# Another order of K chunks behind the norms, two equal column groups for the indexer, and its key's layer norm elsewhere

## The chip, the core and the metric

The kernel runs on one core of a Trainium2 chip. The metric is the device time of one execution in microseconds (us). TensorE (PE) multiplies, VectorE (DVE), ScalarE (ACT) and GpSimd (POOL) do the rest, and SyncE (SP) issues nearly all transfers. The engines run their own instruction lists and meet at semaphores.

## What is computed

Two blocks over 512 positions of width 1024, all in float32. The first has two layers of SwiGLU feed-forward, a mixer (attention variants), cross attention and a second feed-forward. The second block is the one in which two of the three parts of the change lie:

```python
h = rms_norm_2(x, norm_mix_pre[l])
proj = h @ w_in[l]          # split into xr, gr, q, k, v, iq, ik, iw, g_a, g_b
iq = partial_rope(iq.reshape(bsz, s, N_IDX_HEADS, IDX_DIM), IDX_ROT_DIM)   # 512 columns
ik = layer_norm(ik, idx_k_ln_g[l], idx_k_ln_b[l])                          # 64 columns
ik = partial_rope(ik[:, :, None, :], IDX_ROT_DIM)[:, :, 0, :]
iw = iw * idx_w_scale                                                      # 8 columns
y_att = dsa_sparse_attention(q, k, v, iq, ik, iw)
```

Every feed-forward and mixer starts with an RMS norm of x: `y = x * rsqrt(mean(x*x) + EPS) * g`, and the result is the left operand of a matrix product over K = 1024.

## The kernel before

**A matrix product (GEMM)** is done in groups of columns. A group fills four of the eight PSUM banks (jobs 0 to 3, one bank each), and groups alternate between banks 0 to 3 and banks 4 to 7; `home[name, g]` is the first bank (0 or 4) of group g. Each float32 operand is split into a high and a low part, so that each product takes three matmuls: high by high, and the two mixed ones. With K = 1024 a group has 8 steps k of 128, taken in pairs kp; a pair is one weight chunk.

**Weights** come as one stream of chunks (`stream`), in the order in which PE uses them. SP loads a chunk into one of four `raw` buffers, ACT rounds it to `wh`, DVE subtracts to get `wl` (`act_split`, `dve_split`). Both run `AHEAD = 3` chunks before PE, with four buffers, so a split waits until PE has done the chunk four places earlier, and PE waits for `w_lo`, the mark of a finished DVE split.

**A norm in front of a GEMM**: PE transposes the scaled rows of x (tile `xn`) by a product with the identity, so that bank c holds the 128 columns of chunk c for all positions. `pe_turn_x` visits for each of four row tiles first the four banks that the next GEMM starts in, then the other four (`far_first`). ACT then rounds bank c to `hTh` (`act_norm_hi`) and DVE makes `hTl` and marks bank c as drained (`dve_norm_lo`); both take c = 0, 1, ..., 7. The GEMM behind it starts with k = 0; job j writes bank home + j and so waits, beside the operands of step k, until that bank is drained. Eight GEMMs follow a norm this way: `f1u0`, `in0`, `f2u0`, `f1u1`, `in1`, `f2u1`, `idx` and `f3u`. By the number of groups ahead of them, `home` of their first group is 4 for `f1u0`, `f2u0`, `in1`, `f2u1` and `f3u`, and 0 for `in0`, `f1u1` and `idx`.

**The indexer** (`idx`) is two groups: 512 columns (iq) and 72 columns (ik and iw). ACT evicts the first to `tq` and the second to `ti`; POOL applies the rotary embedding (`pool_rope`). Then, at the end of `idx`, PE transposes `tq` (16 transposes of 128 columns, `pe_turn`), and DVE runs the layer norm of ik in `dve_idx`'s `evict`: per row tile statistics, a wait for POOL's power of -0.5 (`pool_rstd`), scale, gain, bias; POOL then does its rotary embedding and turns to the next tile. The next GEMM, `qkv`, has three groups of 512; ik (`ti`) is transposed behind its first group. The weight splits of `qkv` stand on DVE behind the layer norm.

`act_gemm`, `dve_gemm` and `pe_gemm` call `side(g, kp)` after each pair of steps (None: after the group), and `evict(g)` after that. These calls are the places where the other work is put. `handover` makes an engine wait for the end of a phase on all others.

Of the kernel before, what the change touches and what calls it, by code (L numbers as in the profile page):

```python
# [191 lines left out]
def gemm_table(T):  # L192

    def gate_up(name, wg, wu):
        return (name, KD, [[(wg, c, 256, "h", "A"), (wu, c, 256, "h", "A")] for c in range(0, FF, 256)])

    def rows(name, w, K, widths, a="h", form="B", c0=0):
        groups = []  # L200
        for n in widths:
            groups.append([(w, c0, n, a, form)])
            c0 += n
        return (name, K, groups)

    G = []
    for l in range(2):
        wgu = T["ffn1_w_gu"][l]
        G.append(gate_up(f"f1u{l}", wgu[:, 0:FF], wgu[:, FF:2 * FF]))
        G.append(rows(f"f1d{l}", T["ffn1_w_down"][l], KF, [512, 512], "f"))  # L210
        if l == 0:
            w = T["ev_w_in"][0]
            G.append(("in0", KD, [[(w, 0, 512, "h", "B")], [(w, 512, 256, "h", "B")], [(w, 1792, 512, "h", "B")],
                                  [(w, 768, 512, "h", "A")], [(w, 1280, 512, "h", "A")]]))
            G.append(rows("out0", T["ev_w_out"][0], KD, [512, 512]))
        else:
            G.append(rows("in1", T["od_w_in"][0], KD, [512] * 6))
            G.append(rows("out1", T["od_w_out"][0], KD, [512, 512]))
        G.append((f"kv{l}", KD, [[(T["xa_w_kv"][l], c, 512, "m", "B")] for c in (1024, 1536, 0, 512)]))
        G.append(rows(f"xq{l}", T["xa_w_q"][l], KD, [512] * 2))  # L220
        G.append(rows(f"xo{l}", T["xa_w_o"][l], KD, [512] * 2))
        wgu = T["ffn2_w_gu"][l]
        G.append(gate_up(f"f2u{l}", wgu[:, 0:FF], wgu[:, FF:2 * FF]))
        G.append(rows(f"f2d{l}", T["ffn2_w_down"][l], KF, [512, 512], "f"))
    w = T["w_in_2"][0]
    G.append(("idx", KD, [[(w, 3584, 512, "h", "B")], [(w, 4096, 72, "h", "B")]]))
    G.append(rows("qkv", w, KD, [512] * 3, c0=2048))
    G.append(("rnn", KD, [[(w, c, 256, "h", "A"), (w, 1024 + c, 256, "h", "A")] for c in range(0, 1024, 256)]))
    G.append(("ya", KD, [[seg] for c in range(0, 1024, 512)
                         for seg in ((w, 4168 + c, 512, "h", "A"), (T["w_rnn_out_2"][0], c, 512, "y", "A"))]))  # L230
    G.append(rows("gb", w, KD, [512] * 2, form="A", c0=5192))
    G.append(rows("yb", T["w_att_out_2"][0], KD, [512] * 2, form="A"))
    G.append(rows("wo", T["w_o_2"][0], KD, [512] * 2, "y"))
    G.append(gate_up("f3u", T["w_ffn_gate_2"][0], T["w_ffn_up_2"][0]))
    G.append(rows("f3d", T["w_ffn_down_2"][0], KF, [512, 512], "f"))
    return G


def widths(lo, n):
# [16 lines left out]
def program(nc, T, out):  # L256
# [59 lines left out]
    bias_in = [flag(f"bias_in{i}") for i in range(4)]  # L316
    y_out = flag("y_out")


    GEMMS = gemm_table(T)  # L320
    spec = {g[0]: g for g in GEMMS}
    stream = [(segs, kp) for _, K, groups in GEMMS for segs in groups for kp in range(K // 2)]
    first, home = {}, {}
    n, side_ = 0, 0
    for name, K, groups in GEMMS:
        first[name] = n
        n += len(groups) * K // 2
        for g in range(len(groups)):
# [64 lines left out]
    def pe_gemm(pe, name, acts, side=lambda g, kp: None):  # L393
        _, K, groups = spec[name]
        n = first[name]
        for g, segs in enumerate(groups):
            jobs, o = [], 0
            for _, _, width, a, form in segs:
# [3 lines left out]
                else:  # L402
                    jobs += [(A, "B", slice(o, o + width), slice(t * P, (t + 1) * P)) for t in range(A.n // P)]
                o += width
            for block in blocks_of(name, g):
                for u in range(len(block)):
                    pe.wait_ge(w_lo, n + u)
                ks = [(2 * kp + kk, n + kp - block[0], kk) for kp in block for kk in range(2)]
                order = [(k, j) for k in ks for j in range(len(jobs))] if len(block) == 1 else \
                        [(k, j) for j in range(len(jobs)) for k in ks]  # L410
                for (k, m, kk), j in order:
                    A, form, wc, tc = jobs[j]
                    b = home[name, g] + j
# [7 lines left out]
                    M = (wc.stop - wc.start) if form == "B" else A.n  # L421
                    for q, (p0, p1) in enumerate(((Wh, Ah), (Wh, Al), (Wl, Ah)) if form == "A" else
                                                 ((Ah, Wh), (Ah, Wl), (Al, Wh))):
                        ins = pe.matmul(bank[b][:, 0:M], p0, p1, start=k == 0 and q == 0, stop=k == K - 1 and q == 2)
                    full, used = k == K - 1, kk == 1 and j == len(jobs) - 1
                    if full:
                        ins.then_inc(summed, (name, g, j))
                        if used:
# [127 lines left out]
                        ins.also(xn_gone, (N, t % 2))  # L556

    def act_norm_hi(act, N, gain):
        for c in range(KD):
            act.wait_ge(turned, (N, c))  # L560
            act_hi(act, bank[c][:, :], hT(N), c, slice(0, S), h_before.get(N), gain[:, c:c + 1])

    def dve_norm_lo(dve, N, gain):
        for c in range(KD):
# [1191 lines left out]
    def act_idx(act):  # L1756
        handover(act, "sparse")

        def side(g, kp):
            if (g, kp) == (1, None):  # L1760
                act_turned(act, "idx", 0, 4, NT, lambda c: iqT[:, c, :], None)

        def evict(g):
            w, dst = ((512, tq), (72, ti))[g]
            for t in range(NT):
                act.wait_ge(summed, ("idx", g, t))
                act.activation(dst[:, t, 0:w], bank[home["idx", g] + t][:, 0:w], AF.Copy).then_inc(
                    put, ("idx", g, t)).also(drained, ("idx", g, t))
        act_gemm(act, "idx", evict, side)

    def dve_idx(dve):
        handover(dve, "sparse")

        def side(g, kp):
            if (g, kp) == (1, None):
                dve_turned(dve, "idx", 0, 4, NT, lambda c: iqT[:, c, :], None)

        def evict(g):
            if g == 0:
                return  # L1780
            for t in range(NT):
                k = ti[:, t, 0:64]
                dve.wait_ge(put, ("idx", 1, t))
                dve.bn_stats(bn[:, t, 0:6], k).then_inc(step, ("ik stats", t))
                dve.wait_ge(step, ("ik stats", t))
                dve.bn_aggr(bn[:, t, 6:8], bn[:, t, 0:6]).then_inc(step, ("ik mean", t))
                dve.wait_ge(rated, ("ik", t))
                dve.tensor_scalar(k, k, bn[:, t, 6:7], bn[:, t, 8:9], ALU.subtract, ALU.mult).then_inc(step, ("ik norm", t))
                dve.wait_ge(ln_in, 0)
                dve.wait_ge(step, ("ik norm", t))  # L1790
                dve.tensor_tensor(k, k, lng[:, 0, :], ALU.mult).then_inc(step, ("ik gain", t))
                dve.wait_ge(step, ("ik gain", t))
                dve.tensor_tensor(k, k, lng[:, 1, :], ALU.add).then_inc(step, ("ik bias", t))
        dve_gemm(dve, "idx", evict, side)

    def pool_idx(pool):
        handover(pool, "sparse")
# [2 lines left out]
        for t in range(NT):  # L1800
            pool_rope(pool, tq[:, t, :], t, 8, ("idx", 0, t), [(put, ("idx", 0, t))]).then_inc(scaled, ("idx", 0, t))
        for t in range(NT):
            k = ti[:, t, 0:64]
# [4 lines left out]
            pool_rstd(pool, bn[:, t, 7:8], bn[:, t, 8:9], 1.0, ("ik", t))  # L1808
            ins = pool_rope(pool, k, t, 1, ("idx", 1, t), [(step, ("ik bias", t)), (step, ("iw", t))])
# [5 lines left out]
    def pe_idx(pe):  # L1815
        def side(g, kp):
            if (g, kp) == (1, None):
                pe_turn(pe, "idx", 0, tq, 4, NT)
        pe_gemm(pe, "idx", {"h": hT("idx")}, side)
# [14 lines left out]

    def act_qkv(act):
        def side(g, kp):
            if kp is None and g == 0:
                act_turned(act, "idx", 1, 1, NT, lambda c: ikT[:, :], None)
            elif kp is None:
# [10 lines left out]

    def dve_qkv(dve):
        def side(g, kp):
            if kp is None and g == 0:
                dve_turned(dve, "idx", 1, 1, NT, lambda c: ikT[:, :], None)
            elif kp is None:
# [369 lines left out]
    def pe_program(pe):  # L2225
# [23 lines left out]
        pe_idx(pe)  # L2249
        pe_qkv(pe)  # L2250
        pe_rnn(pe)
        pe_ya(pe)
# [201 lines left out]
```

## Time and profile before

| | |
|---|---|
| Median of 3 runs | 3300.27 us (3297.53 to 3303.25) |
| Profiled execution, its own time | 3303.06 us |
| Its span in the trace | 3301.3 us |
| PE, DVE, ACT, POOL busy | 96, 43, 36, 8% |
| Mean granted TensorE clock | 0.982 |
| Read from memory | 286.94 MB, 88 GB/s |

The profile is of one execution. Busy time is what an engine spent inside instructions; an idle time is given with the instruction that ended it (its releaser). Matmul durations overlap, so the pace of PE is the distance from one start to the next. TensorE's clock has two levels, granted 1.00 (2.4 GHz) and 0.50 (1.2 GHz).

### The profile page before, as it was taken

The numbers are of one execution on the slowest core, as the hardware profiler recorded it, in microseconds if no ns is written. First come the engines' busy times: TensorE is split into PE (matmuls) and PEld (weight loads), VectorE is DVE, ScalarE is ACT, GpSimd is POOL, SyncE is SP. The second block draws the span as 40 slices with busy tenths as digits, with TensorE's granted clock in tenths as the row PEclk, the third lists the DMA queues.
The fourth block names the chain that finished last, engine by engine and source line by source line (L and its number), as shares of the span: only waits on it lengthen the run. The fifth ranks groups of instructions, "written<-read, shape, count | busy, mean of one in ns | idle before, by whom it ended". The sixth has DMA issues, their size and how long they took to land.

```text
span 3301.3 us, 37036 instructions
## 1 busy us (share of the span) xinstructions
PE 3169.5 (96%) x14548; PEld 2573.5 (78%) x14548; DVE 1409.7 (43%) x2210; ACT 1190.9 (36%) x1999; POOL 248.7 (8%) x513
## 2 busy tenths in 40 slices
PE   8999997999999999999999999999999998989998
PEld 6888885877888888887867877888887685768887
DVE  3332338554333243333465643332325877443322
ACT  3332327443322233222455533332225637333321
POOL 1000013010000000000310100000132100010000
PEclk9999998999999999999999999999989999989999
DMA  4332230422333223322222412332222230223332
GB/s 144 96 94 98 90 96 1 128 90 64 96 98 100 96 90 94 98 96 83 89 90 71 147 51 83 96 96 98 73 83 77 77 102 20 90 77 96 94 98 71
DMA packets 212607, 291.47 MB, mean 88 GB/s; under 512 B 13872, under 2 KB 135984, under 8 KB 212304
## 3 DMA queue, kind: packets, MB, share of 16 engines
q1 hardware_dynamic: 209792, 279.59, 27.0%
q0 software_dynamic: 2640, 9.50, 0.9%
q8 instruction: 115, 1.88, 0.2%
q14 instruction: 60, 0.49, 0.0%
HBM read 286.94 MB, written 2.10 MB: 88 GB/s over the span
## 4 chain that ended last, share of the span: by engine, by line
PE 84%; ACT 5%; issue 4%; DVE 4%; POOL 2%; DMA 0%; SPq 0%; POOLq 0%; DVEq 0%; ACTq 0%
PE ps L94 82%; PE ps L97 2%; ACT sxPT L100 1%; ACT ocPT L100 1%; DVE hTl L109 1%; ACT L100 0%; ACT sxPb L100 0%; ACT ocPb L100 0%; ACT hTh L100 0%; POOL evQ L142 0%; ACT xn L100 0%; POOL stat L103 0%; ACT wh L100 0%; DVE s_ri L115 0%; POOL s_ri L103 0%
## 5 line engine op out<-in xcount | busy, mean ns | idle before, releaser
L103 DVE TENSOR_TENSOR wl<-raw,wh 128x1024 fp32r<-128x1024 f32 (+1 forms) x530 | 641.0, 1216 | 1250.0 <-ACT wh L100 1245.0
L100 ACT ACTIVATE wh<-raw 128x1024 fp32r<-128x1024 f32 (+1 forms) x530 | 552.4, 1051 | 1360.6 <-PE ps L94 1316.8
L94 PE MATMUL ps<-hTh,wh 128*128 128x512 f32 x2144 | 839.4, 392 | 16.8 <-DVE hTl L109 16.4
L94 PE MATMUL ps<-hTh,wl 128*128 128x512 f32 x2144 | 836.4, 390 | 0.0
L94 PE MATMUL ps<-hTl,wh 128*128 128x512 f32 x2144 | 836.3, 390 | 0.0
L94 PEld LDWEIGHTS ps<-hTh,wh 128*128 128x128 f32 x2144 | 404.0, 188 | 104.9 <-DVE hTl L109 13.7
L94 PEld LDWEIGHTS ps<-hTl,wh 128*128 128x128 f32 x2144 | 404.1, 188 | 84.6 <-issue 1.0
L94 PEld LDWEIGHTS ps<-hTh,wl 128*128 128x128 f32 x2144 | 403.7, 188 | 84.0
L94 PE MATMUL ps<-wh,hTh 128*128 128x512 f32 (+2 forms) x832 | 325.2, 391 | 10.7 <-DVE hTl L109 5.8
L94 PE MATMUL ps<-wh,hTl 128*128 128x512 f32 (+2 forms) x832 | 321.8, 387 | 0.0
L94 PE MATMUL ps<-wl,hTh 128*128 128x512 f32 (+2 forms) x832 | 321.8, 387 | 0.0
L94 PEld LDWEIGHTS ps<-wh,hTh 128*128 128x128 f32 x832 | 161.1, 194 | 42.8 <-DVE hTl L109 6.5
L94 PEld LDWEIGHTS ps<-wh,hTl 128*128 128x128 f32 x832 | 160.9, 193 | 30.8
L94 PEld LDWEIGHTS ps<-wl,hTh 128*128 128x128 f32 x832 | 161.2, 194 | 30.1 <-issue 0.5
L106 POOL TENSOR_SCALAR stat<-stat 128x1 f32<-128x1 f32 x52 | 12.1, 232 | 1726.1 <-ACT f2d0jk L100 366.2
L97 PE MATMUL ps<-misc,xn 128*128 128x128 f32 x352 | 52.0, 303 | 23.0 <-DVE xn L106 14.9
L94 PE MATMUL ps<-wh,f11Fl 128*128 128x512 f32 x176 | 68.5, 389 | 0.0
L94 PE MATMUL ps<-wh,f21Fl 128*128 128x512 f32 x176 | 68.5, 389 | 0.0
L94 PE MATMUL ps<-wh,f20Fl 128*128 128x512 f32 x176 | 68.5, 389 | 0.0
L94 PE MATMUL ps<-wh,f10Fh 128*128 128x512 f32 x176 | 68.5, 389 | 0.0
L94 PE MATMUL ps<-wl,f10Fh 128*128 128x512 f32 x176 | 68.5, 389 | 0.0
L94 PE MATMUL ps<-wh,f10Fl 128*128 128x512 f32 x176 | 68.5, 389 | 0.0
(363 smaller groups left out, 3946.6 us busy)
## 6 DMA issues: line engine op xcount, KB each, us to landing
raw<-in_ffn_w_gu SPq DMA_DIRECT2D x352, 256.0 KB, 3.1
raw<-in_ffn_w_down SPq DMA_DIRECT2D x88, 512.0 KB, 3.5
raw<-in_xa_w_kv SPq DMA_DIRECT2D x32, 512.0 KB, 3.9
raw<-in_w_in SPq DMA_DIRECT2D x32, 512.0 KB, 3.7
raw<-in_od_w_in SPq DMA_DIRECT2D x24, 512.0 KB, 3.6
raw<-in_w_ffn_gate SPq DMA_DIRECT2D x44, 256.0 KB, 2.8
raw<-in_w_ffn_up SPq DMA_DIRECT2D x44, 256.0 KB, 3.1
raw<-in_w_ffn_down SPq DMA_DIRECT2D x22, 512.0 KB, 3.8
```

The source lines that it names most:

```text
L94: return self.made(lambda e: e.matmul(*a, **k))
L97: return self.made(lambda e: e.transpose(*a, **k))
L100: return self.made(lambda e: e.activation(*a, **k))
L103: return self.made(lambda e: e.tensor_tensor(*a, **k))
L106: return self.made(lambda e: e.tensor_scalar(*a, **k))
L109: return self.made(lambda e: e.scalar_tensor_tensor(*a, **k))
```

## The change

Three things are edited.

1. `pair_order` gives the order in which the first group of a GEMM takes its pairs of steps. For the eight named GEMMs the two pairs whose operands lie in the group's own banks come first: with home 4 the order of k is 4, 5, 6, 7, 0, 1, 2, 3, with home 0 it stays. The weight stream, PE and the two norm evictions (`act_norm_hi`, `dve_norm_lo`) use that order.
2. `idx` is two groups of 292 columns. ACT evicts 292 columns of iq after the first; after the second it evicts for each row tile first the 72 columns of ik and iw, then the other 220 of iq. The rotary embedding of iq on POOL so comes after the second group.
3. The layer norm of ik is cut in two and put into `qkv`'s first group: the statistics behind the weight splits of its first chunk, the rest behind those of its third. POOL does the rates of all four row tiles, and then the four rotary embeddings. The 16 transposes of iq move from the end of `idx` into `qkv`'s second group, behind its second chunk.

```diff
@@ gemm_table @@
-    G.append(("idx", KD, [[(w, 3584, 512, "h", "B")], [(w, 4096, 72, "h", "B")]]))
+    G.append(rows("idx", w, KD, [292] * 2, c0=3584))
...
+NORMED = ("f1u0", "in0", "f2u0", "f1u1", "in1", "f2u1", "idx", "f3u")
...
+    def pair_order(name, g, K, at):
+        got = list(range(K // 2))
+        return got[at // 2:at // 2 + 2] + got[:at // 2] + got[at // 2 + 2:] if g == 0 and name in NORMED else got
...
+            stream += [(segs, kp) for kp in pair_order(name, g, K, home[name, g])]
...
+    def chunk_order(name, g):
+        _, K, _ = spec[name]
+        return [2 * kp + kk for kp in pair_order(name, g, K, home[name, g]) for kk in range(2)]
@@ pe_gemm @@
+            ko = chunk_order(name, g)
...
-                ks = [(2 * kp + kk, n + kp - block[0], kk) for kp in block for kk in range(2)]
+                ks = [(ko[2 * kp + kk], n + kp - block[0], kk) for kp in block for kk in range(2)]
...
-                    if k == 0:
+                    if k == ko[0]:
@@ act_norm_hi, dve_norm_lo @@
-        for c in range(KD):
+        for c in chunk_order(N, 0):
@@ act_idx, evict @@
+                if g == 0:
+                    act.activation(tq[:, t, 0:292], b[:, 0:292], AF.Copy).then_inc(drained, ("idx", g, t))
+                else:
+                    act.activation(ti[:, t, 0:72], b[:, 220:292], AF.Copy).then_inc(put, ("idx", 1, t))
+                    act.activation(tq[:, t, 292:512], b[:, 0:220], AF.Copy).then_inc(put, ("idx", 0, t)).also(
+                        drained, ("idx", g, t))
@@ pe_qkv, side (act_qkv and dve_qkv alike with act_turned and dve_turned) @@
+            if (g, kp) == (1, 1):
+                pe_turn(pe, "idx", 0, tq, 4, NT)
@@ dve_qkv, side @@
+            if (g, kp) == (0, 0):
+                dve_idx_stats(dve)
+            if (g, kp) == (0, 2):
+                dve_idx_norm(dve)
```

`dve_idx_stats` and `dve_idx_norm` hold the old instructions of the layer norm, the first two of each tile in the one and the last three in the other, each in a loop over the four row tiles. Five norms are touched in the same way; here is DVE in front of `f2u0`, a GEMM of home 4 (`ps4` is bank 4, `hTl` the low part of the norm's result), before and after:

```order
 L106 TENSOR_SCALAR xn0<-x,stat 128x1024
 L106 TENSOR_SCALAR xn1<-x,stat 128x1024
+L109 SCALAR_TENSOR_TENSOR hTl<-ps4,prm,hTh 128x512
+L109 SCALAR_TENSOR_TENSOR hTl<-ps5,prm,hTh 128x512
+L109 SCALAR_TENSOR_TENSOR hTl<-ps6,prm,hTh 128x512
+L109 SCALAR_TENSOR_TENSOR hTl<-ps7,prm,hTh 128x512
 L109 SCALAR_TENSOR_TENSOR hTl<-ps0,prm,hTh 128x512
 L109 SCALAR_TENSOR_TENSOR hTl<-ps1,prm,hTh 128x512
 L109 SCALAR_TENSOR_TENSOR hTl<-ps2,prm,hTh 128x512
 L109 SCALAR_TENSOR_TENSOR hTl<-ps3,prm,hTh 128x512
-L109 SCALAR_TENSOR_TENSOR hTl<-ps4,prm,hTh 128x512
-L109 SCALAR_TENSOR_TENSOR hTl<-ps5,prm,hTh 128x512
```

The eight evictions are the same ones; banks 4 to 7 now stand in front of banks 0 to 3. The second place is DVE from the norm in front of `idx` to `qkv` (`wl` is a weight split, `s_bn` and `s_ti` the layer norm), before:

```order
L109 SCALAR_TENSOR_TENSOR hTl<-ps,prm,hTh 128x512 x8
L103 TENSOR_TENSOR wl<-raw,wh 128x1024 x2
L103 TENSOR_TENSOR wl<-raw,wh 128x2x72 x4
L103 TENSOR_TENSOR wl<-raw,wh 128x1024 x2
L121 COPY s_iqT<-ps 128x512 x2
L127 BN_STATS s_bn<-s_ti 128x6
L130 BN_AGGR s_bn<-s_bn 128x2
L106 TENSOR_SCALAR s_ti<-s_ti,s_bn 128x64
L103 TENSOR_TENSOR s_ti<-s_ti,s_lng 128x64 x2
...
L103 TENSOR_TENSOR s_ti<-s_ti,s_lng 128x64 x2
L103 TENSOR_TENSOR wl<-raw,wh 128x1024 x5
```

and after it:

```order
L109 SCALAR_TENSOR_TENSOR hTl<-ps,prm,hTh 128x512 x8
L103 TENSOR_TENSOR wl<-raw,wh 128x2x292 x6
L103 TENSOR_TENSOR wl<-raw,wh 128x1024 x4
L127 BN_STATS s_bn<-s_ti 128x6
L130 BN_AGGR s_bn<-s_bn 128x2
...
L103 TENSOR_TENSOR wl<-raw,wh 128x1024 x2
L106 TENSOR_SCALAR s_ti<-s_ti,s_bn 128x64
L103 TENSOR_TENSOR s_ti<-s_ti,s_lng 128x64 x2
...
L103 TENSOR_TENSOR wl<-raw,wh 128x1024
L121 COPY s_ikT<-ps 128x512
```

Four splits of `qkv` (128x1024) stand now ahead of the statistics, where two stood, and two more ahead of the scaling; the copies of iq's transposes (`s_iqT`) have moved behind those of ik (`s_ikT`).

## Rows read from the trace of the kernel before

**Rows 1.** The page, part 1: busy us (share of the span) xinstructions
```profile
PE 3169.5 (96%) x14548; PEld 2573.5 (78%) x14548; DVE 1409.7 (43%) x2210; ACT 1190.9 (36%) x1999; POOL 248.7 (8%) x513
```

**Rows 2.** Timeline, PE around f1u1: start, us, instruction, idle before and releaser
```profile
1176.14 3.32 PE L97 MATMUL ps<-misc,xn 128*128 128x128 f32 x24
...
1181.95 0.50 PE L94 MATMUL ps<-hTh,wh 128*128 128x512 f32 x1 [0.88 <-DVE hTl L109]
...
1184.81 0.39 PE L94 MATMUL ps<-hTh,wh 128*128 128x512 f32 x1
```

**Rows 3.** Timeline, PE and DVE around f2u0
```profile
806.62 3.31 PE L97 MATMUL ps<-misc,xn 128*128 128x128 f32 x24
...
815.57 0.76 PE L94 MATMUL ps<-hTh,wh 128*128 128x512 f32 x1 [4.04 <-DVE hTl L109]
...
819.81 0.39 PE L94 MATMUL ps<-hTh,wh 128*128 128x512 f32 x1
...
818.67 2.36 DVE L103 TENSOR_TENSOR wl<-raw,wh 128x1024 fp32r<-128x1024 f32 x2 [1.27 <-ACT wh L100]
```

**Rows 4.** Timeline, PE around in1, f2u1 and f3u
```profile
1550.11 0.76 PE L94 MATMUL ps<-wh,hTh 128*128 128x512 f32 x1 [4.04 <-DVE hTl L109]
...
1556.07 0.39 PE L94 MATMUL ps<-wh,hTl 128*128 128x512 f32 x1
...
2000.07 0.77 PE L94 MATMUL ps<-hTh,wh 128*128 128x512 f32 x1 [4.04 <-DVE hTl L109]
...
2923.60 3.68 PE L97 MATMUL ps<-misc,xn 128*128 128x128 f32 x16 [1.29 <-DVE xn L106]
2931.00 0.47 PE L94 MATMUL ps<-hTh,wh 128*128 128x512 f32 x1 [3.72 <-DVE hTl L109]
```

**Rows 5.** Timeline, DVE, PE and ACT around f1u0, at the kernel's start
```profile
16.44 5.36 DVE L109 SCALAR_TENSOR_TENSOR hTl<-ps,prm,hTh 128x512 fp32r<-128x512 f32 x8
...
19.98 0.77 PE L94 MATMUL ps<-hTh,wh 128*128 128x512 f32 x1 [3.73 <-DVE hTl L109]
...
30.54 3.90 ACT L100 ACTIVATE wh<-raw 128x1024 fp32r<-128x1024 f32 x4 [8.42 <-POOL la L106]
...
33.01 0.50 PE L94 MATMUL ps<-hTh,wh 128*128 128x512 f32 x1 [0.34 <-DVE wl L103]
```

**Rows 6.** Windows of PE: stretch, us, busy us (count), granted clock, DMA
```profile
409.07:414.82 5.75, 5.75 (x49) 1.00 0.18 42
2388.32:2392.03 3.71, 3.71 (x35) 1.00 0.29 61
2392.16:2405.18 13.02, 13.02 (x64) 0.50 0.33 101
```

**Rows 7.** The chain that ended last, in order of time: start, us, what
```profile
1181.95 359.37 PE ps L94 x1584
...
2461.18 1.75 PE ps L97 x16
```

**Rows 8.** Timeline, PE in idx and qkv
```profile
2366.39 0.50 PE L94 MATMUL ps<-wh,hTh 128*128 128x512 f32 x1 [0.88 <-DVE hTl L109]
...
2424.00 0.80 PE L94 MATMUL ps<-wh,hTh 128*128 128x512 f32 x1 [4.00 <-DVE wl L103]
...
2437.68 0.60 PE L97 MATMUL ps<-misc,s_ti 128*128 128x128 f32 x4
2439.15 0.47 PE L94 MATMUL ps<-wh,hTh 128*128 128x512 f32 x1 [0.88 <-DVE s_ikT L121]
```

**Rows 9.** Timeline, DVE and POOL in the layer norm of ik
```profile
2414.75 0.32 DVE L106 TENSOR_SCALAR s_ti<-s_ti,s_bn 128x64 f32<-128x64 f32 x1 [2.44 <-POOL s_bn L103]
...
2415.66 0.68 POOL L103 TENSOR_TENSOR s_rt<-s_ti,misc 128x8 f32<-128x8 f32 x4 [0.95 <-DVE s_ti L103]
...
2417.17 0.24 POOL L106 TENSOR_SCALAR s_iw<-s_ti 128x8 f32<-128x8 f32 x1
...
2422.88 4.54 POOL L103 TENSOR_TENSOR s_rt<-s_ti,misc 128x8 f32<-128x8 f32 x4 [0.95 <-DVE s_ti L103]
```

More of the change, by code:

```diff
@@ L317, in program @@
     y_out = flag("y_out")
+    def pair_order(name, g, K, at):
+        got = list(range(K // 2))
+        return got[at // 2:at // 2 + 2] + got[:at // 2] + got[at // 2 + 2:] if g == 0 and name in NORMED else got
     GEMMS = gemm_table(T)
     spec = {g[0]: g for g in GEMMS}
-    stream = [(segs, kp) for _, K, groups in GEMMS for segs in groups for kp in range(K // 2)]
-    first, home = {}, {}
-    n, side_ = 0, 0
+    first, home, stream = {}, {}, []
+    side_ = 0
     for name, K, groups in GEMMS:
-        first[name] = n
-        n += len(groups) * K // 2
-        for g in range(len(groups)):
+        first[name] = len(stream)
+        for g, segs in enumerate(groups):
             side_ ^= 1
             home[name, g] = 4 * side_
+            stream += [(segs, kp) for kp in pair_order(name, g, K, home[name, g])]
     def last_chunk(name):
@@ L423, in pe_gemm @@
                                                  ((Ah, Wh), (Ah, Wl), (Al, Wh))):
-                        ins = pe.matmul(bank[b][:, 0:M], p0, p1, start=k == 0 and q == 0, stop=k == K - 1 and q == 2)
-                    full, used = k == K - 1, kk == 1 and j == len(jobs) - 1
+                        ins = pe.matmul(bank[b][:, 0:M], p0, p1, start=k == ko[0] and q == 0, stop=k == ko[-1] and q == 2)
+                    full, used = k == ko[-1], kk == 1 and j == len(jobs) - 1
                     if full:
@@ L563, in dve_norm_lo @@
     def dve_norm_lo(dve, N, gain):
-        for c in range(KD):
+        for c in chunk_order(N, 0):
             dve.wait_ge(turned, (N, c))
@@ L1757, in act_idx @@
         handover(act, "sparse")
-        def side(g, kp):
-            if (g, kp) == (1, None):
-                act_turned(act, "idx", 0, 4, NT, lambda c: iqT[:, c, :], None)
         def evict(g):
-            w, dst = ((512, tq), (72, ti))[g]
             for t in range(NT):
+                b = bank[home["idx", g] + t]
                 act.wait_ge(summed, ("idx", g, t))
-                act.activation(dst[:, t, 0:w], bank[home["idx", g] + t][:, 0:w], AF.Copy).then_inc(
-                    put, ("idx", g, t)).also(drained, ("idx", g, t))
@@ L1769, in act_idx @@
-        act_gemm(act, "idx", evict, side)
+                if g == 0:
[4 more added lines that the diff above has]
+                        drained, ("idx", g, t))
+        act_gemm(act, "idx", evict)
@@ L1771, in dve_idx @@
     def dve_idx(dve):
         handover(dve, "sparse")
[L1774 to L1793, printed above, removed]
@@ L1794, in dve_idx, with dve_idx_stats, dve_idx_norm @@
-        dve_gemm(dve, "idx", evict, side)
+        dve_gemm(dve, "idx", none)
+    def dve_idx_stats(dve):
+        for t in range(NT):
+            dve.wait_ge(put, ("idx", 1, t))
+            dve.bn_stats(bn[:, t, 0:6], ti[:, t, 0:64]).then_inc(step, ("ik stats", t))
+            dve.wait_ge(step, ("ik stats", t))
+            dve.bn_aggr(bn[:, t, 6:8], bn[:, t, 0:6]).then_inc(step, ("ik mean", t))
+    def dve_idx_norm(dve):
+        for t in range(NT):
+            k = ti[:, t, 0:64]
+            dve.wait_ge(rated, ("ik", t))
+            dve.tensor_scalar(k, k, bn[:, t, 6:7], bn[:, t, 8:9], ALU.subtract, ALU.mult).then_inc(step, ("ik norm", t))
+            dve.wait_ge(ln_in, 0)
+            dve.wait_ge(step, ("ik norm", t))
+            dve.tensor_tensor(k, k, lng[:, 0, :], ALU.mult).then_inc(step, ("ik gain", t))
+            dve.wait_ge(step, ("ik gain", t))
+            dve.tensor_tensor(k, k, lng[:, 1, :], ALU.add).then_inc(step, ("ik bias", t))
@@ L1808, in pool_idx @@
             pool_rstd(pool, bn[:, t, 7:8], bn[:, t, 8:9], 1.0, ("ik", t))
+        for t in range(NT):
+            k = ti[:, t, 0:64]
             ins = pool_rope(pool, k, t, 1, ("idx", 1, t), [(step, ("ik bias", t)), (step, ("iw", t))])
@@ L1812, in pool_idx @@
             pool.tensor_copy(ti[:, t, 64:128], k).then_inc(scaled, ("idx", 1, t))
[L1815 to L1819, printed above, removed]
     qkv_buf = [tq2, tq, tq2]
@@ L1836, in side @@
         def side(g, kp):
+            if (g, kp) == (1, 1):
+                act_turned(act, "idx", 0, 4, NT, lambda c: iqT[:, c, :], None)
             if kp is None and g == 0:
@@ L1852, in side @@
         def side(g, kp):
+            if (g, kp) == (0, 0):
+                dve_idx_stats(dve)
+            if (g, kp) == (0, 2):
+                dve_idx_norm(dve)
+            if (g, kp) == (1, 1):
+                dve_turned(dve, "idx", 0, 4, NT, lambda c: iqT[:, c, :], None)
             if kp is None and g == 0:
@@ L2248, in pe_program @@
         handover(pe, "sparse")
-        pe_idx(pe)
+        pe_gemm(pe, "idx", {"h": hT("idx")})
         pe_qkv(pe)
```

1 line of the change is left out of this document (removed).

## The prediction

> **What bounds the kernel now.** I read the page's busy shares first: PE is busy 96% of the span [rows 1], so time can be won only where PE idles, runs at half clock, or does work that could be shorter. Then I read the chain in order of time for the long stretches of PE, and between them the timeline of PE for its idle times and their releasers. In a long stretch 1584 matmuls of 512 columns take 359.37 us [rows 7], 0.2269 us each; nothing in the change alters those. What it touches are the joints: five norms in front of a GEMM of home 4, and the indexer.
>
> **The norms.** f1u1 is a GEMM of home 0, and shows what a joint costs when evictions are taken in the order in which banks are turned and needed: from the first transpose of the next-to-last batch (1176.14) to the 13th matmul (1184.81) 8.67 us, PE idle 0.88 us ahead of the first matmul, full pace after it [rows 2]. f2u0 has home 4. PE's first matmul there writes bank 4, and DVE drains banks 0 to 3 first: idle 4.04 us, and then 12 matmuls take 4.24 us (815.57 to 819.81) where f1u1's take 2.86, because PE comes back at half clock. The same distance is 13.19 us [rows 3]. The change gives f2u0 the order of f1u1 with the two halves of the banks exchanged, so I price it as f1u1: 13.19 - 8.67 = **4.5 us**. f2u1 has the same idle of 4.04 [rows 4]: **4.5**. in1 too has 4.04, but its slow stretch is longer: 14 matmuls from 1550.11 to 1556.07 take 5.96 us [rows 4] instead of 14 x 0.2269 = 3.18. Against f2u0 (1.38 us lost) it loses 2.78, 1.4 more: **5.8** with f1u1's own small excess taken off.
>
> f3u: idle 3.72 behind 16 transposes at a half-clock pace (3.68 us) [rows 4]. With bank 4 first, ACT and DVE can start when the ninth of these 16 is done instead of the 13th, 4 x 0.23 = 0.9 earlier, and the first needed bank is the first and no longer the fifth of DVE's evictions, 4 x 0.67 (5.36 for 8 [rows 5]) = 2.7 earlier. PE then starts about 3.6 us earlier, hardly idle. Of the slow start behind it (1.4 to 2.8 us where rows show one) between nothing and all may go, since PE now comes to the matmuls from transposes without a gap. I take 1.0: **4.6**, bounds 3.6 and 6.
>
> Is the next thing late? PE holds two chunks, 48 matmuls or 10.9 us, at each joint. At f2u0 DVE's split of the third ends 818.67 + 1.2 = 819.9 [rows 3], now 0.4 earlier with the norm. PE, restarted at about 812.4, needs it at 823.3. Slack 3.9 us, and the same at in1, f2u1 and f3u by the same row order. There is no new wait.
>
> f1u0 is different. DVE's evictions begin at 16.44 in either version, behind two weight splits. PE can begin at 17.25 (0.8 behind, as in f1u1) instead of 19.98 [rows 5]. But the third chunk is split only after a chain of small POOL instructions (the recurrence's constants): ACT at 30.54, released by POOL, and PE's matmul at 33.01 [rows 5]. That chain starts when DVE has finished all eight evictions, which is no earlier now. So PE comes 2.7 us earlier to the same wait. It would be done with 48 matmuls near 28.4 and idle 4.6 us instead of 0.34, and behind idle times of 3.7 to 4.04 us rows show a slow start that costs 1.4 to 2.8. The early start buys nothing: **-1.7**, bounds 0 and -2.8.
>
> **The indexer, first part.** Before, from 2366.39 (first matmul) to 2439.15 (first of qkv's second group) [rows 8] are 72.76 us. The 72-column group starts at 0.11 us a matmul, and after 3.7 us PE's clock falls to 0.50 and stays there for 13 us [rows 6], so that the group costs 16.9 us for a seventh of the columns.
>
> Rebuild it. No matmul of 292 columns is in the trace. The nearest rows are 256 columns, 48 in 5.75 us or 0.1198 each at a granted clock of 1.00 [rows 6], and 512 at 0.2269 [rows 7]. On the line between them 292 takes 0.1198 + 36 x 0.000418 = 0.1349. Bounds: 0.1198 (as 256) and 0.227 (as 512). I take 0.135, as it is so near to 256. The first step k waits for DVE's evictions, 0.67 us a bank: its fourth job starts at 2366.39 + 3 x 0.67 = 2368.40 and 183 matmuls are left, 24.7 us, to 2393.1. qkv's first group: 96 x 0.2269 = 21.8, to 2414.9. The four transposes of ik and the wait for DVE's copy stay, 1.47 us (2437.68 to 2439.15) [rows 8]. The second group so begins at 2416.3: 22.8 us earlier. The 16 transposes of iq are now inside it, at 1.75 us at full clock [rows 7]. Net **21.1 us**.
>
> The Trainium skill has another price for the matmul (TensorE: Matmul & The Clock Gate, section "Wait — 56ns, not 53.3ns?"): columns over 2.4 GHz plus about 2.5 ns once the clock is up. This trace doesn't agree: 512 columns over 2.4 GHz are 213.3 ns, and it shows 226.9 [rows 7], 13.6 more. By the page 292 would take 124 ns, and 192 of them 2.0 us less than in my sum.
>
> **The indexer, moved work.** Before, PE waited 4.00 us at 2424.00 for a weight split that stood behind the layer norm on DVE [rows 8], where DVE and POOL take turns (DVE idle 2.44 us for POOL in one tile) [rows 9]. Now the splits stand first. DVE's statistics come behind the splits for chunk four of qkv at about 2397, POOL's four rates are done by 2403, and the scaling begins behind the next split but one. PE finishes the second chunk of qkv at 2393.1 + 10.9 = 2404.0, ACT and DVE take 2.4 more, so the scaling begins near 2406.5, at some 0.8 us a tile. POOL's part of a tile is 1.51 (2415.66 to 2417.17) [rows 9]: the last is ready at 2407.3 + 4 x 1.51 = 2413.4. PE wants it at 2414.9. Cover 1.5 us, so I price the move at nothing. If the cover is gone PE waits for POOL, microsecond for microsecond, and over about 3.7 us of idling also a slow start.
>
> One of POOL's groups of four took 4.54 us instead of 0.68 [rows 9], while DVE did four splits in a row (the last released PE at 2424.00). The new place has one split beside POOL, so I keep 0 to 3 us for it. The Trainium skill names the cause (GPSIMD Engine Reference, section 1, Specifications): POOL's path to SBUF is shared with VectorE, with contention for DVE instructions of two SBUF inputs, as a weight split is. By that rule moving the norm next to splits is wrong; the price above is taken from the row.
>
> ACT's evictions of 220 and 72 columns and SP's smaller transfers (299 KB for 3.2 us of PE, instead of 512 KB for 5.4) are hidden by PE's matmuls. The third chunk of idx is the tight one: its split waits for the end of the norm, and is there near 2372.6 for a PE that needs it at 2373.8. Without that cover it costs what it is late, under 1 us.
>
> **The sum.** 4.5 + 4.5 + 5.8 + 4.6 - 1.7 + 21.1 = 38.8 us. The profiled execution took 3303.06, so it would take 3264.3; the median of the runs is 2.8 below the profiled one, and I put the gain to the median: 3300.27 - 38.8 = **3261.5**. PE is the bound in the long stretches behind each joint, so what is won at a joint shifts all that follows.
>
> **Rivals.**
> - *PE waits for the moved layer norm.* For: cover of 1.5 us, and the group of 4.54. Against: only one split beside it. 3 us of waiting and 2.8 of half clock: 3267. Chance 0.12.
> - *The clock falls in the 292-column groups,* as it did in the 72-column one. Against: 5.75 us of 256 columns held 1.00 [rows 6]; the indexer has 26 us of it. From 3.7 us on at half clock, 292 columns over 1.2 GHz are 0.243, and 22 us become 40: 18 us lost, 3280. Chance 0.05.
> - *The reordering doesn't give what it says:* as at f1u0, another wait ends last at the other four joints. Against: slack of 3.9 us. The 19.4 us go and the indexer stays: 3281. Chance 0.06.
> - *Slower.* POOL is held by DVE for its whole indexer work, from 2388 to the last rotary embedding. That is 25 us with its waits in my timetable; the one group was stretched 6.7 times. DVE's scaling waits for POOL's rates, with the splits of qkv queued behind it, so PE stops. Stretched 6.7 times it ends at 2556 instead of by 2415, and the time is 3261.5 + 141 = 3402. It decides from a stretch of 2.6 times (38.8 us late). Against: DVE's splits are 1.2 us in every 5.4. Chance 0.02.
> - *The forecast,* 3256 to 3267: chance 0.70. The rest, 0.05, lies just outside it.
>
> **How the numbers follow.** The bounds of the terms give 34 to 43 us (f3u 3.6 to 6, f1u0 0 to -2.8, 292 columns by the page's figure, 0 to 3 for POOL), and the place of half-clock stretches shifts between executions by a microsecond or two each: 3256 to 3267. With the first rival and some of the others the range that should hold 8 in 10 is 3253 to 3272. A measurement of this kernel can tell about 0.2%, 6.6 us, from no change. All cases but the last are faster by more than that: faster 0.96, within 0.2% 0.02, slower 0.02.
>
> **What would show it.** Idle 0.9 us or less at f2u0, in1 and f2u1, with full clock behind it; under 1 at f3u; at f1u0 an idle of 4 to 5 us ahead of the third chunk. Matmuls of 292 columns 0.135 us apart at 1.00, and 23 us less between idx's first matmul and qkv's second group. No idle of PE for a weight split in qkv, and ik's transposes right behind its first group. It is wrong if PE stands there for POOL, if the granted clock is 0.50 in idx, or if the long stretches are not shifted but stretched.

## Result and profile after

The changed kernel takes **3264.53 us** (median of 4 runs, 3259.60 to 3265.56) against 3301.38 of the kernel before (four runs, three of them those of the table of before): ratio 0.9887, 95% interval 0.9870 to 0.9904, or 36.9 us less. The prediction was 3261.5 (3253 to 3272). The profiled execution was the fastest of the four: 3259.60, span 3257.8.

The page of the changed kernel, part 1, for [rows 1]:

```profile
PE 3144.9 (97%) x14548; PEld 2553.7 (78%) x14548; DVE 1408.9 (43%) x2210; ACT 1191.1 (37%) x2003; POOL 248.4 (8%) x513
```

The number of matmuls is the same and PE is still busy nearly all the time. It is busy 24.6 us less. Most of that was half clock: the clock's records add up to 122.8 us of it before and 81.5 after, and half of the difference is 20.6. The rest of the gain, 43.5 - 24.6 = 18.9 us of the span, was idle time. The waits of PE, one line of the kernel before and the same one of after (engine, what it waited for, us in total, times, longest):

```profile
PE ps L94 <- DVE hTl L109: 22.2, 8, 4.0
```

```profile
PE ps L94 <- DVE hTl L109: 6.8, 8, 1.1
```

All eight norms are in this line. Here are four of them, PE in the changed kernel around f2u0, in1, f2u1 and f3u, for [rows 3, 4]:

```profile
803.57 3.31 PE L97 MATMUL ps<-misc,xn 128*128 128x128 f32 x24
...
809.37 0.50 PE L94 MATMUL ps<-hTh,wh 128*128 128x512 f32 x1 [0.88 <-DVE hTl L109]
...
812.25 0.40 PE L94 MATMUL ps<-hTh,wh 128*128 128x512 f32 x1
...
1539.43 0.50 PE L94 MATMUL ps<-wh,hTh 128*128 128x512 f32 x1 [0.88 <-DVE hTl L109]
...
1542.78 0.39 PE L94 MATMUL ps<-wh,hTl 128*128 128x512 f32 x1
...
1984.07 0.50 PE L94 MATMUL ps<-hTh,wh 128*128 128x512 f32 x1 [0.88 <-DVE hTl L109]
...
2885.17 3.44 PE L97 MATMUL ps<-misc,xn 128*128 128x128 f32 x16 [1.29 <-DVE xn L106]
2888.99 0.51 PE L94 MATMUL ps<-hTh,wh 128*128 128x512 f32 x1 [0.38 <-DVE hTl L109]
```

Idle is 0.88 us at three of them and 0.38 at f3u, and the first matmul takes 0.50 us, not 0.76: full clock. From transpose to 13th matmul f2u0 now takes 812.25 - 803.57 = 8.68 us, as f1u1 did in [rows 2] (8.67), where it was 13.19.

The start of the kernel, PE around f1u0, for [rows 5]:

```profile
17.14 0.77 PE L94 MATMUL ps<-hTh,wh 128*128 128x512 f32 x1 [1.10 <-DVE hTl L109]
...
20.69 0.56 PE L94 MATMUL ps<-hTh,wl 128*128 128x512 f32 x1
...
32.80 0.50 PE L94 MATMUL ps<-hTh,wh 128*128 128x512 f32 x1 [2.67 <-DVE wl L103]
```

PE begins 2.8 us earlier, and gets the third chunk at 32.80, where it got it at 33.01. The first nine matmuls run at half clock (17.14 to 20.69), as the first seven did before (19.98 to 22.67, from 0.77 us in [rows 5] on).

The indexer, a window of PE (stretch, us, busy us and count, granted clock, DMA share, GB/s), the timeline of PE behind it, and the chain (start, us, what), for [rows 6 to 8]:

```profile
2349.12:2375.50 26.38, 26.38 (x192) 1.00 0.53 146
```

```profile
2397.41 0.60 PE L97 MATMUL ps<-misc,s_ti 128*128 128x128 f32 x4
2398.88 0.47 PE L94 MATMUL ps<-wh,hTh 128*128 128x512 f32 x1 [0.88 <-DVE s_ikT L121]
```

```profile
2349.12 48.45 PE ps L94 x288
...
2410.03 1.75 PE ps L97 x16
```

No idle time and full clock from idx's first matmul through qkv's first group: 288 matmuls in one piece of the chain. From 2349.12 to 2398.88 are 49.76 us instead of 72.76. The 16 transposes of iq take their 1.75 us at 2410.03.

**Where the time went.** I take the distance between the starts of the same two matmuls in both profiles, us:

| stretch | before | after | predicted gain | gain |
|---|---|---|---|---|
| f1u0, start to third chunk | 25.44 | 25.29 | -1.7 | 0.2 |
| f2u0 | 15.93 | 11.41 | 4.5 | 4.5 |
| in1 | 16.77 | 10.97 | 5.8 | 5.8 |
| f2u1 | 13.16 | 8.72 | 4.5 | 4.4 |
| f3u | 19.71 | 14.60 | 4.6 | 5.1 |
| indexer, to behind iq's transposes | 90.26 | 69.05 | 21.1 | 21.2 |
| sum | | | 38.8 | 41.2 |

The rest of the program is the same within 0.6 us in each long piece, except for block 1 between f1u0's third chunk and f2u0: 773.61 before, 770.78 after, 774.34 in a second profile of the changed kernel.

### The profile page after: what moved, and what is told of

Same layout as the page of the kernel before. It is cut to its first block, busy times and chain, and to the rows that moved or that the text cites. A ratio compares the mean times of both kernels' runs of the same rounds, so it can differ in the third digit from the quotient of the medians.

```text
span 3257.8 us, 37053 instructions
## 1 busy us (share of the span) xinstructions
PE 3144.9 (97%) x14548; PEld 2553.7 (78%) x14548; DVE 1408.9 (43%) x2210; ACT 1191.1 (37%) x2003; POOL 248.4 (8%) x513
## 4 chain that ended last, share of the span: by engine, by line
PE 85%; ACT 5%; issue 4%; DVE 3%; POOL 2%; DMA 0%; POOLq 0%; DVEq 0%; ACTq 0%
PE ps L94 83%; PE ps L97 2%; ACT ocPT L100 1%; ACT sxPT L100 1%; ACT hTh L100 1%; ACT L100 0%; ACT ocPb L100 0%; ACT xn L100 0%; POOL stat L103 0%; ACT sxPb L100 0%; ACT wh L100 0%; POOL evQ L142 0%; DVE s_ri L115 0%; POOL s_ri L103 0%; POOL evPb L142 0%
## 5 line engine op out<-in xcount | busy, mean ns | idle before, releaser
L94 PE MATMUL ps<-wh,hTh 128*128 128x512 f32 (+2 forms) x832 | 317.2, 381 | 3.5 <-DVE hTl L109 2.6
L94 PE MATMUL ps<-wh,hTl 128*128 128x512 f32 (+2 forms) x832 | 314.5, 378 | 0.0
L94 PE MATMUL ps<-wl,hTh 128*128 128x512 f32 (+2 forms) x832 | 314.4, 378 | 0.0
```

The source lines that it names most:

```text
L94: return self.made(lambda e: e.matmul(*a, **k))
```

## Experiments

All medians are beside runs of the kernel before on the same chip (3301.17 to 3301.46). "After" is the changed kernel.

**The two halves of the change apart.** First the order of K alone, with `idx` and `qkv` as before; then the indexer alone:

```diff
@@ norms_only: gemm_table; idx and qkv functions of the kernel before @@
-    G.append(rows("idx", w, KD, [292] * 2, c0=3584))
+    G.append(("idx", KD, [[(w, 3584, 512, "h", "B")], [(w, 4096, 72, "h", "B")]]))
@@ idx_only @@
-NORMED = ("f1u0", "in0", "f2u0", "f1u1", "in1", "f2u1", "idx", "f3u")
+NORMED = ()
```

> The first part of the change alone: the order of K chunks behind the norms; the indexer as before. Theory (the joints add up, PE bounds what lies between): the profiles of before and after give 4.5 (f2u0), 5.8 (in1), 4.5 (f2u1) and 5.0 (f3u) us, and f1u0 between 0.2 and -2.8; together 17 to 20 us less than before, near 3283, and after = before minus this gain minus that of the indexer alone. Rival (a joint's gain is given back later, and the indexer's part carries more than its 21 us): under 12 us less, above 3289.

> The indexer's two parts alone (groups of 292, layer norm and transposes moved), every norm evicted in the old order. Theory: 21 us less than before, 3279 to 3282, and from the first matmul of idx to qkv's second group the same 23 us less as in the changed kernel. Rival (the joints carry more): under 16 us less, above 3285.

The order alone: 3282.90 us (3281.62 to 3284.55), ratio 0.9946 [0.9933, 0.9958], 18.6 less. The indexer alone: 3280.44 (3277.70 to 3281.71), ratio 0.9938 [0.9926, 0.9950], 21.0 less. Both as expected. Their sum, 39.6, is the 36.9 to 38.2 measured for both together (this result and the one of `after_again` below), within the intervals of some 4 us each. The profiles say it more sharply: each stretch of the table is as long with its part alone as with both, within 0.15 us (`norms_only` at the five norms, `idx_only` in the indexer). So the gains add up.

**The changed kernel once more, and without f1u0 in the order.**

```diff
@@ no_f1u0 @@
-NORMED = ("f1u0", "in0", "f2u0", "f1u1", "in1", "f2u1", "idx", "f3u")
+NORMED = ("in0", "f2u0", "f1u1", "in1", "f2u1", "idx", "f3u")
```

> The changed kernel once more, for its time beside the others on one chip and for a second profile. Theory: 36 to 39 us less than before. The profiled execution of after lay 5 us below its median; if the place of half-clock stretches is what differs, this profile shows them at other joints (f1u0, the first block's mixer, f3u), with the same idle times of PE, and a sum of half-clock time above the 81.5 us of the first profile by twice what it is slower. Rival: an idle time differs.

> The changed kernel, but f1u0 takes its chunks in the old order. Theory of the prediction: PE comes to f1u0's third chunk no earlier than it can be split, so the new order there buys nothing and leaves a longer idle that may bring a slow start; this kernel is 0 to 2.8 us faster than the changed one. Rival (what the profile of after shows: third chunk at 32.80 instead of 33.01, clock not lowered behind an idle of 2.67): the same within 0.3 us.

The repetition: 3263.22 us (3263.20 to 3263.51), ratio 0.9886 [0.9871, 0.9901]. Its idle times at the joints are those of the first profile; the difference of the spans (3261.5 and 3257.8) is nearly all in block 1 (3.6 us). As a sum, only 3.3 us more of half clock lie against it, where half clock alone would need twice the 3.7. The matmuls' starts show where it is, in the first block's mixer. Behind two idle times that are equal in both profiles (1.17 or 1.18, and 2.17 us), the clock stayed at 1.00 in the first and fell to 0.50 for 6.8 us in the second (from 417.3): 2.4 us. The other 1.1 lie between 496 and 604 us, where PE once idled 4.77 us for DVE instead of 1.52 (at 572) and other pieces were shorter. Why these differ is open. Without f1u0: 3261.31 (3259.36 to 3263.59), 0.9881 [0.9867, 0.9894]. The runs overlap, and the third chunk comes at 25.70 us after the first matmul of the kernel, where after and its repetition have 25.29 and 25.45. The median without it is 1.9 us below the repetition's and 3.2 below the first result, the way the prediction had it, but in the profile the third chunk is not earlier. So f1u0's new order is worth nothing that these runs can tell, in either direction.

**Which half of the reordering matters.** Two things changed together: the order in which the norm's banks are emptied, and the order in which PE wants their contents. Each alone:

```diff
@@ evict_order_only: stream and pe_gemm in natural order, evictions as in after @@
-            stream += [(segs, kp) for kp in pair_order(name, g, K, home[name, g])]
+            stream += [(segs, kp) for kp in range(K // 2)]
-            ko = chunk_order(name, g)
+            ko = list(range(K))
@@ k_order_only: act_norm_hi and dve_norm_lo in natural order, PE as in after @@
-        for c in chunk_order(N, 0):
+        for c in range(KD):
```

> The changed kernel, but only ACT's and DVE's evictions of the norms take the new order; weights and PE take k = 0, 1, ... as before. Theory (a joint needs both: the bank that the first job writes and the operand of its first step must be the same eviction): at f2u0, in1 and f2u1 the banks are free early, but the operand of k = 0 is DVE's fifth eviction, so PE idles 0.88 + 4 x 0.67 = 3.6 us, with a slow start; 15 to 20 us slower than the changed kernel. Rival (the bank alone is what PE waits for): idle 0.88 and the same time as the changed kernel.

> The other half: weights and PE take k = 4 to 7 first where home is 4, the evictions stay 0, 1, ..., 7. Theory: bank 4 and the operand of k = 4 are both the fifth eviction, so nothing is gained over the kernel before at the five norms: idle 4.04 us at f2u0, in1 and f2u1, 3.7 at f3u; 16 to 21 us slower than the changed kernel. Rival (the order of k alone frees PE): idle of 0.88 and the time of the changed kernel.

The evictions alone: 3278.43 us (3277.23 to 3279.91), 0.9933 [0.9918, 0.9948]. K alone: 3280.06 (3277.32 to 3281.27), 0.9935 [0.9918, 0.9952]. They are 14 to 15 and 16 to 17 us slower than after, at the lower end of what was expected or a little under it, and about where the version without any reordering is (3280.44). PE at f2u0 with DVE's row, the evictions alone; then K alone:

```profile
810.83 5.36 DVE L109 SCALAR_TENSOR_TENSOR hTl<-ps,prm,hTh 128x512 fp32r<-128x512 f32 x8 [1.22 <-PE ps L97]
...
814.27 0.61 PE L94 MATMUL ps<-hTh,wh 128*128 128x512 f32 x1 [3.51 <-DVE hTl L109]
```

```profile
813.17 5.36 DVE L109 SCALAR_TENSOR_TENSOR hTl<-ps,prm,hTh 128x512 fp32r<-128x512 f32 x8 [1.66 <-ACT hTh L100]
...
816.61 0.50 PE L94 MATMUL ps<-hTh,wh 128*128 128x512 f32 x1 [3.95 <-DVE hTl L109]
```

In the first the bank is free and the operand of k = 0 is missing (DVE's fifth eviction); in the second the operand is there and the bank is not. Both waits end with the same engine's fifth eviction: it begins 4 x 0.67 us into DVE's row, at 813.5 and 815.9, and PE's matmul follows 0.8 us behind that. Only an eviction that frees the bank and delivers the operand at once ends both. (The 0.50 us of the second row is no full clock for long: the next eight matmuls but one take 0.57 to 0.63 us.)

**The indexer's two causes.** The old widths with the moved layer norm and transposes:

```diff
@@ old_widths: gemm_table, and ACT evicts 512 and 72 columns @@
-    G.append(rows("idx", w, KD, [292] * 2, c0=3584))
+    G.append(("idx", KD, [[(w, 3584, 512, "h", "B")], [(w, 4096, 72, "h", "B")]]))
```

> The changed kernel with the indexer's groups at 512 and 72 columns again; layer norm and transposes stay in their new places. Theory (two separate causes): the 72-column group costs its 17 us again with the clock at half, against 13 for a group of 292, and the first costs 21.8 against 12.8; the wait for the weight split (4.0 and its slow start) stays away. So 11 to 15 us slower than the changed kernel. What the clock does behind the 72 columns is open: if it is still low in qkv's first matmuls, up to 1.5 us more. Rival (the gain is that of the moved layer norm, the widths matter little): under 5 us slower.

3276.36 us (3271.93 to 3277.73), ratio 0.9922 [0.9910, 0.9935]: 12 to 13 us slower than after. Windows of PE in idx, old widths:

```profile
2354.35:2376.29 21.94, 21.94 (x97) 1.00 0.33 83
2376.29:2380.56 4.27, 4.27 (x41) 1.00 0.39 107
2381.60:2391.57 9.97, 9.97 (x49) 0.50 0.38 107
```

The 512-column group holds full clock. The 72-column group has it too in the second row, at 0.11 us a matmul; its starts stay 0.11 apart for 48 matmuls, until 2381.56, 5.3 us in all. Then they are 0.21 apart at 0.50, although PE never idles in the whole stretch: the same picture as in [rows 6], also with nothing else of the old layout around it. In the stretch of the table the old widths take 81.66 us. So 90.26 - 81.66 = 8.6 us of the indexer's gain come from the moved layer norm and transposes, and 81.66 - 69.05 = 12.6 from the widths. About half of the latter is half clock: 48 matmuls of 72 columns at 0.213 instead of 0.111 are 4.9 us, and qkv's first sixteen take 5.34 us instead of 3.67. The other 6 us are there at full clock: 72 columns, a quarter of 292, take 0.111 us and not a quarter of 0.133.

**The cover of the moved layer norm.** The scaling one chunk later:

```diff
@@ ln_late: dve_qkv, side @@
-            if (g, kp) == (0, 2):
+            if (g, kp) == (0, 3):
                 dve_idx_norm(dve)
```

> The changed kernel with the scaling part of ik's layer norm one chunk later, behind the weight splits of qkv's fourth chunk (5.44 us later). POOL's last rotary embedding was ready at 2396.55, PE took it at 2397.41: cover 0.86 us. Theory (the cover is what is left, beyond it PE waits microsecond for microsecond): PE idles 4.5 to 4.7 us at ik's transposes, and loses 0 to 2.8 us more at half clock; 4.5 to 7.5 us slower. Rival (there is more cover than that, or the weight splits behind catch it): under 2 us slower.

3268.31 us (3266.73 to 3271.06), ratio 0.9901 [0.9887, 0.9914], some 4 to 5 us slower than after; the indexer's stretch is 5.6 longer. The loss is at the lower end of the expected one and made up differently: qkv's second group starts 3.7 us later and not 4.5 to 4.7, and then loses 1.9 at half clock. PE behind qkv's first group, and a window behind it:

```profile
2399.03 0.27 PE L97 MATMUL ps<-misc,s_ti 128*128 128x128 f32 x1
2400.07 0.33 PE L97 MATMUL ps<-misc,s_ti 128*128 128x128 f32 x1 [0.77 <-POOL s_ti L121]
2401.45 0.48 PE L97 MATMUL ps<-misc,s_ti 128*128 128x128 f32 x1 [1.05 <-POOL s_ti L121]
2402.83 0.47 PE L97 MATMUL ps<-misc,s_ti 128*128 128x128 f32 x1 [0.90 <-POOL s_ti L121]
2404.18 0.76 PE L94 MATMUL ps<-wh,hTh 128*128 128x512 f32 x1 [0.88 <-DVE s_ikT L121]
```

```profile
2404.18:2408.20 4.02, 4.02 (x10) 0.50 0.43 127
```

This is the first rival of the prediction, brought about: PE waits for POOL tile by tile (2.7 us in three waits and one transpose at a time), and the group behind starts at half clock. How near the changed kernel is to it shows POOL there:

```profile
2377.09 3.17 POOL L103 TENSOR_TENSOR s_rt<-s_tq,misc 128x64 f32<-128x64 f32 x4
...
2382.60 1.16 POOL L106 TENSOR_SCALAR s_bn<-s_bn 128x1 f32<-128x1 f32 x1
...
2393.66 1.22 POOL L103 TENSOR_TENSOR s_ti<-s_rt 128x8 f32<-128x8 f32 x2
...
2396.31 0.24 POOL L121 COPY s_ti<-s_ti 128x64 f32<-128x64 f32 x1
```

ik is ready at 2396.31 + 0.24 = 2396.55 and PE turns to it at 2397.41: a cover of 0.86 us. The third row costs 1.22 us where its neighbours take 0.36, the first 3.17 where they take 1.16, and the second, a single small instruction, 1.16 where they take 0.19. All three lie beside weight splits on DVE, and end as the split ends or just behind it (2380.26 and 2379.80, 2383.76 and 2383.72, 2394.88 and 2394.66). DVE's rows, without the split of the second (2382.49, 1.23 us):

```profile
2377.31 2.49 DVE L103 TENSOR_TENSOR wl<-raw,wh 128x1024 fp32r<-128x1024 f32 x2 [5.47 <-ACT wh L100]
...
2389.07 0.31 DVE L106 TENSOR_SCALAR s_ti<-s_ti,s_bn 128x64 f32<-128x64 f32 x1
...
2393.38 1.28 DVE L103 TENSOR_TENSOR wl<-raw,wh 128x1024 fp32r<-128x1024 f32 x1 [0.99 <-ACT wh L100]
```

In `ln_late` no split stands beside POOL's part, no group of it is stretched, and ik is ready 4.6 us later and not the full 5.44. The 0.84 between them is the stretch of the third row, and that is why PE waited less than expected.

**What holds the third chunk at f1u0.** The recurrence's constants, a chain of small instructions over DVE, ACT and POOL, stand ahead of that chunk's split. Put behind f1u0's GEMM:

```diff
@@ rec_later: ACT's list; DVE and POOL alike @@
         act_norm(act, "f1u0", None)
-        act_recurrence(act)
         for l, C in enumerate(crosses):
...
             act_ffn_up(act, f1)
+            if l == 0:
+                act_recurrence(act)
```

> The changed kernel with the recurrence's small constants computed behind f1u0 instead of in front of it. Theory (the chain of small POOL instructions ends last at f1u0's third chunk): its split then follows the norm at once, PE's idle of 2.67 us there is gone, and the earlier start of f1u0 is kept: 2.7 us faster than the changed kernel, more by up to 2.8 where that one had a slow start. Rival (the next thing, loads of weights or the splits themselves, ends at the same time): under 1 us faster.

**3254.61 us** (3254.33 to 3260.01), ratio 0.9864 [0.9849, 0.9879]: the lowest median of all, 9 to 10 us below after, where 2.7 to 5.5 were expected. PE and ACT at f1u0, and a window of PE:

```profile
17.22 0.47 PE L94 MATMUL ps<-hTh,wh 128*128 128x512 f32 x1 [1.18 <-DVE hTl L109]
...
21.77 2.96 ACT L100 ACTIVATE wh<-raw 128x1024 fp32r<-128x1024 f32 x3 [2.31 <-issue]
```

```profile
17.22:28.24 11.02, 11.02 (x48) 1.00 0.49 155
```

ACT splits the third chunk at 21.77 instead of 30.33, and PE runs through: the 49th matmul starts at 28.24. That is 4.6 us earlier than in after, so the chain of constants was what made PE's early start worthless. Of the 4.6, 2.7 are the idle time, and 1.9 come from full clock in the first matmuls, which after did not have; `both_more` below begins in the same way, has the clock at 0.50 from 18.6 to 22.0, and is only 2.9 us shorter than after at this joint. The other 4 to 5 us of the medians are not at this joint. The span of the profiled execution is 5.2 us shorter than after's, 4.5 of it at this joint, and 8.9 shorter than its repetition's, 4.7 at this joint and 3.3 in the rest of block 1; whether the moved chain or the scatter between executions gives the rest stays open. 2.7 of the 3.3 are in the two places of the mixer that differ between after and its repetition as well, which speaks for the scatter.

**Both, with ik's transposes later too.** The stop of 1.47 us ahead of qkv's second group remains in all versions so far. ("The kernel before" in the next expectation is `rec_later`.) Here ik is transposed in qkv's third group:

```diff
@@ both_more: rec_later, and in pe_qkv, act_qkv, dve_qkv @@
-            if kp is None and g == 0:
+            if (g, kp) == (2, 1):
                 pe_turn(pe, "idx", 1, ti, 1, NT)
```

> As the kernel before, and ik's transposes moved into qkv's third group, behind its second chunk, where bank 4 is free. Theory: PE's idle of 0.88 us for DVE's copy goes as well, and the cover for POOL grows by 27 us; 0.9 us faster than the kernel with the later constants, 3.5 to 6.5 faster than the changed one. Rival (the copy only moves the wait to another place): the same as with the later constants alone.

3256.20 us (3254.22 to 3256.88), ratio 0.9862 [0.9849, 0.9876]. The indexer's stretch is 68.38 us instead of 69.03, and PE no longer stands behind the transposes; 0.65 us can't be told in the medians. I would take or leave this edit by the simplicity of the code alone.

## Why the prediction was right, and where it was not

**f2u0, in1, f2u1: right to 0.1 us each.** f1u1, which had the wanted order by the chance of its home, was a full model of the joint, and the change made the others equal to it, half clock included. The two single halves show that the mechanism is the one named: with either half missing, the fifth eviction of DVE still ends the wait.

**f3u: 4.6 predicted, 5.1 measured, within its bounds 3.6 to 6.** The idle went from 3.72 to 0.38, as worked out. I gave the slow start behind it 1.0 of 1.4 to 2.8 us; with the first matmul at 0.51 us it went whole, and that is the 0.5.

**f1u0: -1.7 predicted, 0.2 measured.** Here a term was mis-sized. The wait was right: PE comes earlier to the same third chunk. The price of half clock was not. I let PE do its 48 matmuls at full pace (17.25 to 28.4) and idle 4.6 us, with the loss behind it. But the nine first matmuls ran at half clock, inside time that was idle anyway, the idle was 2.67 and not 4 to 5, and the clock behind it full. The sign was in my own row: the 0.77 us of the first matmul in [rows 5] is a half-clock matmul. Other executions show the other course, in a kernel with the same start (`ln_late`):

```profile
17.29:20.50 3.21, 3.21 (x14) 1.00 0.82 265
32.99:36.00 3.01, 3.01 (x7) 0.50 0.54 166
```

```profile
32.99 0.80 PE L94 MATMUL ps<-hTh,wh 128*128 128x512 f32 x1 [4.55 <-DVE wl L103]
```

There it began fast (14 matmuls in 3.21 us), idled 4.55 and came back at half clock: 7 matmuls in 3.01 us, 1.4 more than 7 x 0.2269. So the predicted course exists, at 1.4, inside the bounds of 0 to -2.8. `old_widths` took it too (idle 4.57, 1.4 us lost), while `norms_only` and `after_again` went as after did (idle 2.62 and 2.61). Which of the two an execution takes is not in my hands; over these five profiles the term is some -0.5, and its upper bound of 0 was missed by 0.2.

**The indexer: 21.1 predicted, 21.2 measured.** The pace of 292 columns was the largest unknown. In the trace the starts are 0.133 us apart (2374.80, 2374.94, 2375.07), against 0.135 drawn between 256 and 512 columns; idx takes 26.48 us to qkv's first matmul at 2375.60, predicted 26.7. From the Trainium skill's figure (TensorE: Matmul & The Clock Gate, "Wait — 56ns, not 53.3ns?"), columns over 2.4 GHz plus about 2.5 ns, comes an estimate of 124 ns, and the measurement doesn't agree with it here. The end of the group was met as well: PE wanted ik 48.29 us after idx's first matmul, predicted 48.5.

**The moved layer norm at no price: right, with less cover than I said.** The scaling began 39.95 us after idx's first matmul (predicted 40.1), ik was ready at 47.43 (predicted 47.0), and the cover was 0.86 us, not 1.5. Of the missing 0.6, 0.4 is ik being ready later, and it would have been 0.4 early without the 0.86 lost by the stretched POOL group of 1.22 us; 0.2 is PE wanting it earlier. The Trainium skill's rule (GPSIMD Engine Reference, section 1, Specifications) is that POOL shares its way to SBUF with VectorE, with contention for DVE instructions of two SBUF inputs. The rows beside splits agree: the POOL groups there take 2.7, 3.4 and 6 times as long. The rows beside the layer norm's gain and bias, DVE instructions of 128x64 with two SBUF inputs too, do not: POOL takes 0.69 and 0.74 us there, against 0.68. It cost nothing because the stretch lay inside the cover; `ln_late` shows the price when the cover is gone, 5.6 us for one chunk. It also shows half clock behind four waits of 0.77 to 1.05 us, where the prediction had put a slow start only behind some 3.7 us of idling.

**The third chunk of idx** came in time: 26.38 busy of 26.38 us.

**The rivals.** The clock did not fall in 26 us of 292 columns. The reordering gave what it said at four of five joints, and the fifth was the one named. POOL was held for three single groups, not for its whole work. One reading behind these rivals was wrong: the group of 4.54 us ran beside four splits in a row, but it was the first of these and not the last that released PE at 2424.00 (they run from 2422.72 to 2427.36). The price taken from the group doesn't depend on it.

**From sum to median.** Gains of 41.2 us in the profiles became 36.9 and 38.2 in the medians. The before of the profiles was 3303.06, 1.6 above its median of 3301.46 beside the repetition; and between the joints the changed kernel's second profile lost 0.7 in block 1 and 0.5 behind f2u0 (0.4 of it between in1 and f2u1). That leads from 41.2 to 38.4, where the repetition measured 38.2. The other median lies 1.3 higher, less than its own runs are apart. So the 38.8 came out near the medians with two errors of opposite sign: f1u0 and f3u were priced 2.4 us too low, and the sum was taken over to the median as if nothing else moved, 2.8 us too much. (The prediction's terms add up to 43.9 us at their upper end, not to the 43 that it gives.)

## What to carry to other kernels

When an engine must both empty a buffer for the next stage and prepare that stage's operand, let the same step do both for what is wanted first; one of the two orders alone gives almost nothing (21 to 23 us of 37, and that is the indexer's share). Look in the same trace for a place that has the wanted order by chance: here it priced three joints to 0.1 us, the slow clock behind them included. And when a wait only moves behind the next one, as at f1u0, ask what holds the next one; taking that away was worth 2.9 and 4.5 us at the joint in two profiles, and the reordering alone 0.2.

## What the hardware showed beyond expectation

- PE busy without a gap can be throttled: 72-column matmuls ran at 1.00 for 5.3 us in `old_widths` and `norms_only` and 3.8 in the kernel before, then at 0.50. Matmuls of 292 columns held 1.00 for 26.38 us. The same 584 columns cost 12.6 us less in two equal groups.
- The length of an idle time alone does not say what the clock does behind it. Behind 2.61 and 2.67 us at f1u0 it was at 1.00 (0.50 us for the first matmul); behind 2.64 us in `k_order_only` (at 2565.05) it was at 0.50, and behind the 2.17 us in the first block's mixer it was either. At the joints, behind 3.5 to 4.6 us, it fell to 0.50 in every profile, before PE came back or within 0.6 us behind (0.4 behind the 3.72 in front of f3u before, 0.6 behind the 3.95 in `k_order_only`).
- A POOL group of small tensors beside a two-input DVE instruction was stretched 2.7 times (1.16 to 3.17 us), 3.4 times (0.36 to 1.22) and 6 times (0.19 to 1.16), each beside a weight split. Groups beside DVE's gain and bias of 128x64, which have two inputs too, took their usual 0.69 and 0.74 us.
- Executions of the same kernel differ by up to 6 us (3259.60 and 3265.56). In the two that were profiled (3259.60 and 3263.20) the idle times at the joints are equal; the difference lay in the first block's mixer, 2.4 us of it in one stretch of half clock.
